# Mixture-of-experts stage of a two-layer transformer block: expert blocks of 64 slots on two column groups replaced by blocks of 32 slots on four

## The reference

```python
g_sel = argmax(tok @ gw + gb)                     # one of 4 groups
top_v, top_i = lax.top_k(e_logits of that group, 2)
w_sel = softmax(top_v) * p_g                      # two experts per token, 16 experts in all
for e in range(16):
    gu = tok @ w_gu[e]                            # 1024 -> 2 x 512
    act = silu(gu[:, :512]) * gu[:, 512:]
    y = y + combine[:, e:e + 1] * (act @ w_down[e])   # 512 -> 1024
```

| layer | tokens of experts 0 to 15 | blocks of 64 | blocks of 32 |
|---|---|---|---|
| 0 | 104, 55, 102, 67, 40, 60, 57, 45, 102, 93, 117, 70, 26, 34, 29, 23 | 23 | 40 (4,2,4,3,2,2,2,2,4,3,4,3,1,2,1,1) |
| 1 | 57, 30, 38, 21, 57, 29, 23, 71, 14, 19, 19, 16, 28, 20, 36, 34 | 17 | 23 (2,1,2,1,2,1,1,3,1,1,1,1,1,1,2,2) |

## Time and profile before

### The profile page before, as it was taken

The page is one execution under the profiler, slowest core; times in us unless marked ns, Lnnn a source line. Parts: engine busy times, 40 slices in busy tenths (PEclk is TensorE's granted clock), DMA queues, the critical chain, the costliest instruction groups (busy, mean ns, idle before and its releaser), DMA issues. The chain is left out here.

```text
span 1308.4 us, 15199 instructions
## 1 busy us (share of the span) xinstructions
PE 1125.2 (86%) x5396; PEld 575.0 (44%) x5397; DVE 289.6 (22%) x841; ACT 307.9 (24%) x732; POOL 145.8 (11%) x201
## 2 busy tenths in 40 slices
PE   5899999999996799879999469999995887888672
PEld 3344646656873333223333146666683322322220
DVE  1100064466115100000000051035715100000003
ACT  3211034454234011000111153125624100010002
POOL 0010033000000211111111110012000311111001
PEclk9999999999999799899999879999998998999997
DMA  9872548563406589999899841300047799999983
GB/s 350 299 278 111 229 157 315 212 246 130 193 1 265 170 311 330 352 391 365 323 334 354 312 156 65 118 11 1 1 193 284 268 329 394 390 376 393 394 358 112
DMA packets 92972, 322.89 MB, mean 247 GB/s; under 512 B 10954, under 2 KB 14068, under 8 KB 86644
## 3 DMA queue, kind: packets, MB, share of 16 engines
q1 hardware_dynamic: 70624, 279.19, 55.9%
q0 software_dynamic: 8032, 28.84, 6.7%
q10 hardware_dynamic: 14260, 14.10, 3.2%
HBM read 299.04 MB, written 23.07 MB: 246 GB/s over the span
## 5 line engine op out<-in xcount | busy, mean ns | idle before, releaser
L771 PE MATMUL psum<-weights,R 128*64 128x512 f32 x1280 | 309.9, 636 | 71.3 <-DMA weights<-in_exp_w_gu_dram 54.1
L771 PEld LDWEIGHTS psum<-weights,R 128*64 128x64 f32 x1280 | 100.1, 145 | 253.4 <-issue 253.0
L788 PE MATMUL psum<-weights,lat 128*64 128x512 f32 x592 | 135.2, 599 | 4.3 <-ACT lat L1093 4.3
L478 PE MATMUL psum<-hT,weights 128*128 128x512 f32 (+3 forms) x384 | 135.0, 511 | 2.4 <-ACT hT L935 2.4
L1503 DVE TENSOR_TENSOR lat<-lat,psum 128x256 f32<-128x256 f32 x42 | 17.7, 421 | 527.5 <-ACT lat L1089 527.5
L478 PEld LDWEIGHTS psum<-hT,weights 128*128 128x128 f32 (+1 forms) x384 | 68.5, 182 | 66.4 <-issue 57.5
L1089 ACT ACTIVATE lat<-psum 128x256 f32<-128x256 f32 x42 | 16.1, 383 | 311.5 <-PE psum L771 303.6
L1682 POOL COPY R<-R 64x1024 f32<-64x1024 f32 x40 | 41.3, 1032 | 400.0 <-PE psum L760 220.5
L1300 DVE TENSOR_REDUCE st<-psum 128x1 f32<-128x512 f32 (+1 forms) x96 | 56.9, 600 | 76.5 <-PE psum L588 36.0
L788 PEld LDWEIGHTS psum<-weights,lat 128*64 128x64 f32 x592 | 39.2, 136 | 70.6 <-issue 63.4
L1003 ACT ACTIVATE R<-psum,st 128x512 f32<-128x512 f32 (+1 forms) x78 | 48.0, 616 | 85.8 <-DVE st L1300 42.8
(11 more groups left out here) (224 smaller groups left out, 1081.8 us busy)
## 6 DMA issues: line engine op xcount, KB each, us to landing
weights<-in_exp_w_gu_dram SPq DMA_DIRECT2D x64, 2048.0 KB, 16.9
weights<-in_exp_w_down_dram SPq DMA_DIRECT2D x30, 2048.0 KB, 13.8
...
```

What stands on the lines that cost most here:

```text
L478: mm = nc.tensor.matmul(t[p0:p0 + m, lo:hi], w[:, k, col:col + m], hT[:, k, lo:hi], start=(k == 0), stop=(k == KD - 1))
L771: mm = nc.tensor.matmul(gu_ps[64 * j:64 * j + 64, :], xgT[:, k, :], w_gu[place][:, k, j, :, :], start=(k == 0), stop=(k == KD - 1), skip_g ...
L788: mm = nc.tensor.matmul(y_ps[64 * j:64 * j + 64, :], actT[:, kk % 2, (kk // 2) * 64:(kk // 2) * 64 + 64], w[kk][:, j * 512:(j + 1) * 512], ...
```

## The change

The block size becomes 32 slots, and each matmul of the expert stage uses one of four column groups of 32 with 256 moving columns in place of one of two groups with 512. The slots of a block are gathered as 128 pieces of 1 KB (a quarter of a row for each of the 128 partitions) instead of 64 rows of 4 KB; for this ACT writes the rows to `h_rows` in a permuted order. The gathered tile goes straight into one DVE transpose of 32x32 blocks, which gives `xgT`; POOL's copy, PE's transposes and DVE's copy out of PSUM go. The product of SiLU and up goes through a second DVE transpose in place of PE's two transposes and ACT's copy. The stores become four DMAs of 32 rows of 1 KB per block. PE now waits for `y_copied` and `act_ready` by name. Here is the diff, cut to its core:

```diff
@@ -38,7 +38,9 @@
-BLK = 64
+BLK = 32
+MORE = NTOK // BLK - 1
+QUADS = P // BLK
@@ -104,10 +106,12 @@
-put("more", np.tile(BLK * np.arange(1, 8) + 1, (P, 1)))
-put("count", np.tile(np.arange(BLK), (P, 1)))
+put("more", np.tile(BLK * np.arange(1, MORE + 1) + 1, (P, 1)))
+put("count", np.tile(np.arange(64), (P, 1)))
+put("place", np.tile(np.arange(P) % BLK, (P, 1)))
+put("quad", np.arange(P)[:, None] // BLK)
...
-    put(f"token{layer}", np.tile(np.arange(P)[:, None] + P * np.arange(tiles)[None], (1, 2)))
+    put(f"token{layer}", QUADS * np.tile(np.arange(P)[:, None] + P * np.arange(tiles)[None], (1, 2)))
@@ -173,7 +177,8 @@
-w_gu = [W[i][:, 0:8 * D].rearrange("p (k c h n) -> p k h c n", k=KD, c=2, h=2) for i in range(2)]
+w_gu = [W[i][:, 0:8 * D].rearrange("p (k c b j r) -> p k j c b r", k=KD, c=2, b=4, j=QUADS) for i in range(2)]
@@ -210,9 +215,10 @@
-xg_in = [R1[0:BLK, i * D:(i + 1) * D] for i in range(2)]
-xg = R1[0:BLK, 2 * D:3 * D]
-xgT = part(R1, 3 * D, KD * BLK, "p (k s) -> p k s", k=KD)
+xg = [part(R1, i * 256, 256) for i in range(2)]
+xgT = part(R1, 2 * 256, KD * BLK, "p (k s) -> p k s", k=KD)
@@ -229,9 +235,9 @@
-y_sb = [part(lat, i * 512, 512) for i in range(2)]
-silu_g, act_rows = (part(lat, 1024 + i * 256, 256) for i in range(2))
...
+y_sb = [part(lat, i * 256, 256) for i in range(2)]
+silu_g, act_rows = (part(lat, 512 + i * P, P) for i in range(2))
+actT = part(lat, 768, P, "p (b s) -> p b s", b=4)
@@ -270,18 +276,18 @@
-place_hot = part(lat, 0, 8 * BLK, "p (i s) -> p i s", i=8)
-block_id = part(lat, 8 * BLK, 8 * COLS, "p (i b) -> p i b", i=8)
+place_hot = part(lat, 0, 8 * P, "p (i s) -> p i s", i=8)
+block_id = part(lat, 3 * NTOK, 8 * COLS, "p (i b) -> p i b", i=8)
...
-slots = sb("slots", [BLK, COLS], I32)
-slot_col = sb("slot_col", [BLK, 2], I32)
+slots = sb("slots", [P, COLS], I32)
+slot_col = sb("slot_col", [P, 2], I32)
@@ -733,7 +739,8 @@
-mm = nc.tensor.matmul(t[0:BLK, 0:COLS], place_hot[:, i, :], block_id[:, i, :], start=(i == 0), stop=(i == 2 * nt - 1))
+mm = nc.tensor.matmul(t[:, 0:COLS], place_hot[:, i, :], block_id[:, i, :],
+                      start=(i == 0), stop=(i == 2 * nt - 1))
@@ -745,68 +752,52 @@
+for bank in (1, 3):
...
-def turn_x(g):
...
+gu_ps, y_ps = psum[:, 1, :], psum[:, 3, :]
+x_ready, act_ready, actT_ready = sem(f"x_ready{L}"), sem(f"act_ready{L}"), sem(f"actT_ready{L}")
+gu_done, y_done, y_copied = sem(f"gu_done{L}"), sem(f"y_done{L}"), sem(f"y_copied{L}")
+def gate_up(g, place, landed=None):
+    pe.wait_ge(act_ready, g + 1)
...
-        mm = nc.tensor.transpose(xt_ps[:, k * BLK:(k + 1) * BLK], xg[:, k * P:(k + 1) * P], ident[0:BLK, 0:BLK])
...
-        for j in range(2):
-            mm = nc.tensor.matmul(gu_ps[64 * j:64 * j + 64, :], xgT[:, k, :], w_gu[place][:, k, j, :, :],
+        for j in range(QUADS):
+            mm = nc.tensor.matmul(gu_ps[BLK * j:BLK * j + BLK, 0:256], xgT[:, k, :], w_gu[place][:, k, j, :, :, :],
...
-def turn_act(g):
...
-    for c in range(2):
-        mm = nc.tensor.transpose(at_ps[:, c * P:(c + 1) * P], act_rows[:, c * P:(c + 1) * P], ident)
...
+    pe.wait_ge(y_copied, g + 1)
+    pe.sem_inc(sem("pe_hold"), 1)
...
-        for j in range(2):
-            mm = nc.tensor.matmul(y_ps[64 * j:64 * j + 64, :],
...
+    for b in range(4):
+        for j in range(QUADS):
+            mm = nc.tensor.matmul(y_ps[BLK * j:BLK * j + BLK, 0:256], actT[:, b, :], w[b][:, j * 256:(j + 1) * 256],
+                                  start=(b == 0), stop=(b == 3), skip_group_check=True)
...
-turn_x(0)
...
+    n_blocks = pe.value_load(tabs[L][0:1, ds(pair * 2 + (T_NB + par), 1)], min_val=1, max_val=MORE + 1)
...
-    turn_x(start + 1)
...
-    turn_act(start)
@@ -818,9 +809,7 @@
-turn_x(g + 1)
...
-turn_act(g)
@@ -833,10 +822,9 @@
+pe.sem_inc(gu_done, 1)
@@ -1065,8 +1053,10 @@
-copy(S, rows[:, tt, half * 512:half * 512 + 512], ("hr", L, tt, half),
-     keys=[("h_tile", L, tt)] if half else [])
+src = read(act, "hr", L, tt, half)
+a(rows[:, tt, :].rearrange("p (a k r) -> p k a r", a=QUADS, k=KD)[:, 4 * half:4 * half + 4, :, :],
+  src.rearrange("p (k a r) -> p k a r", k=4, a=QUADS), ACT.Copy)\
+    .then_inc(*mark(S, ("read", "hr", L, tt, half), *([("h_tile", L, tt)] if half else [])))
@@ -1081,43 +1071,36 @@
+y_done, y_copied = sem(f"y_done{L}"), sem(f"y_copied{L}")
...
-    a(actT[:, :, :].rearrange("p c s -> p (c s)"), psum[:, 2, 0:256], ACT.Copy).then_inc(actT_ready, 1)
+    a(silu_g, psum[:, 1, 0:P], ACT.Silu).then_inc(silu_ready, 1)
...
-    a(y_sb[par], psum[:, 3, :], ACT.Copy).then_inc(y_copied, 1)
...
-    for j in range(2):
-        act.dma_start(y_rows[ds(n * BLK - BLK, BLK), j * 512:(j + 1) * 512], y_sb[par][64 * j:64 * j + 64, :])\
+    act.wait_ge(sem(f"y_stored{par}{L}"), ((n + 1) >> 1) * (16 * QUADS))
+    a(y_sb[par], psum[:, 3, 0:256], ACT.Copy).then_inc(y_copied, 1)
+    act.wait_ge(y_copied, n + 1)
+    for j in range(QUADS):
+        act.dma_start(y_rows[ds(n * BLK - BLK, BLK), j * 256:(j + 1) * 256], y_sb[par][BLK * j:BLK * j + BLK, :])\
...
+    act.sem_inc(sem(f"y_stored{par}{L}"), 16 * QUADS)
+act.sem_inc(y_copied, 1)
@@ -1448,9 +1431,9 @@
-step(tt_(cmp7[:, :, :], e16[:, 0, :].unsqueeze(2).to_broadcast([P, 16, 7]),
...
-step(red(e16[:, 1, :], cmp7[:, :, :], AX.X, ALU.add))
+step(tt_(more_of[:, :, :], e16[:, 0, :].unsqueeze(2).to_broadcast([P, 16, MORE]),
+         C("more").unsqueeze(1).to_broadcast([P, 16, MORE]), ALU.is_ge))
+step(red(e16[:, 1, :], more_of[:, :, :], AX.X, ALU.add))
@@ -1465,10 +1448,10 @@
-step(ts(spos_t[:, 1, 0:n2], spos[:, 0:n2], 6, None, ALU.logical_shift_right))
+step(ts(spos_t[:, 1, 0:n2], spos[:, 0:n2], 5, None, ALU.logical_shift_right))
...
-tt_(place_hot[:, 0:n2, :], spos_f[:, 0, 0:n2].unsqueeze(2).to_broadcast([P, n2, BLK]),
-    C("count")[:, 0:BLK].unsqueeze(1).to_broadcast([P, n2, BLK]), ALU.is_equal)
+tt_(place_hot[:, 0:n2, :], spos_f[:, 0, 0:n2].unsqueeze(2).to_broadcast([P, n2, P]),
+    C("place").unsqueeze(1).to_broadcast([P, n2, P]), ALU.is_equal)
@@ -1477,7 +1460,7 @@
-nc.vector.tensor_copy(slots[:, :], t[0:BLK, 0:COLS]).then_inc(*mark(S, ("read", "st", L), ("slots", L)))
+ts(slots[:, :], t[:, 0:COLS], C("quad"), None, ALU.add).then_inc(*mark(S, ("read", "st", L), ("slots", L)))
@@ -1487,22 +1470,36 @@
-    return nc.vector.tensor_copy(xgT[:, :, :].rearrange("p k s -> p (k s)"), psum[:, 0, :]).then_inc(x_ready, 1)
+x_ready, gu_done, silu_ready = sem(f"x_ready{L}"), sem(f"gu_done{L}"), sem(f"silu_ready{L}")
+act_ready, actT_ready, y_done = sem(f"act_ready{L}"), sem(f"actT_ready{L}"), sem(f"y_done{L}")
+def x_turn(par):
+    nc.vector.transpose(xgT[:, :, :].rearrange("p k s -> p (k s)"), xg[par]).then_inc(x_ready, 1)
+def block(g, par):
+    v.wait_ge(sem(f"gathered{1 - par}{L}"), ((g + 1) >> 1) * 16 + 16)
+    v.sem_inc(sem("v_hold"), 1)
+    v.wait_ge(gu_done, g + 1)
+    x_turn(1 - par)
+    v.wait_ge(silu_ready, g + 1)
+    tt_(act_rows, silu_g, psum[:, 1, P:2 * P], ALU.mult).then_inc(act_ready, 1)
+    if not isinstance(g, int) or g:
+        v.wait_ge(y_done, g)
+        v.sem_inc(sem("v_hold"), 1)
+    v.wait_ge(act_ready, g + 2)
+    nc.vector.transpose(actT[:, :, :].rearrange("p b s -> p (b s)"), act_rows).then_inc(actT_ready, 1)
+    v.wait_ge(actT_ready, g + 1)
...
+v.sem_inc(act_ready, 1)
+v.wait_ge(sem(f"gathered0{L}"), 16)
+x_turn(0)
+block(0, 0)
+block(1, 1)
+with v.Fori(1, (total + 1) >> 1) as pair:
...
+        block(pair * 2 + par, par)
@@ -1663,44 +1660,33 @@
+x_ready, col_ready = sem(f"x_ready{L}"), sem(f"col_ready{L}")
+h_parts = h_rows[L].rearrange("t (a c) -> (t a) c", a=QUADS)
...
+def gather(g, par):
...
+    g_.indirect_dma_start(xg[par], None, h_parts, bass.IndirectOffsetOnAxis(ap=slot_col[:, par:par + 1], axis=0))\
...
-def pass_on(g, par):
...
-    nc.gpsimd.tensor_copy(xg, xg_in[par]).then_inc(x_rows, 1)
...
-gather(1, 1, xg_in[1])
+gather(0, 0)
+gather(1, 1)
...
-gather(2, 0, xg_in[0])
-pass_on(1, 1)
-gather(3, 1, xg_in[1])
...
+pairs = (total + 1) >> 1
+with g_.Fori(0, pairs) as pair:
...
-        pass_on(pair * 2 + par, par)
-        gather(pair * 2 + (par + 2), par, xg_in[par])
-pass_on(pairs * 2 - 2, 0)
-pass_on(pairs * 2 - 1, 1)
+        g_.wait_ge(x_ready, pair * 2 + (par + 1))
+        g_.sem_inc(sem("hold"), 1)
+        gather(pair * 2 + (par + 2), par)
...
+    g_.wait_ge(sem(f"gathered{par}{L}"), pairs * 16 + 16)
+for par in range(2):
+    g_.wait_ge(sem(f"y_stored{par}{L}"), ((total + (1 - par)) >> 1) * (16 * QUADS) + 16 * QUADS)
```

More of the change, by code:

```diff
@@ L272, in hybrid_block @@
         r16 = sb("r16", [P, 6, 4, 16])
-        cmp7 = sb("cmp7", [P, 16, 7])
+        more_of = sb("more_of", [P, 16, MORE])
         e16 = sb("e16", [P, 5, 16])
@@ L746, in experts @@
             def experts(L):
-                for bank in range(4):
+                for bank in (1, 3):
                     pe.wait_ge(*at(*last_read[bank]))
-                xt_ps, gu_ps, at_ps, y_ps = (psum[:, b, :] for b in range(4))
```

(24 more changed lines are left out.)

40 lines of the change are left out of this document (removed).

## The result

The changed kernel takes 1257.68 us in the median of four runs (1254.14 to 1259.81), beside 1312.61 for the kernel before: a ratio of 0.9577, interval 0.9543 to 0.9611. The profiled execution took 1259.81 us, its span is 1258.0 (1308.4 before).

What follows compares the result with a forecast made beforehand. Layer 0 was taken as mostly PE-bound, layer 1 as bound by weight loads. Gains of 16.0 and 5.4 less 2.0, 0.5 and 2.0 gave 17 us: span 1308.4 to 1291.5, median 1295.4, range 1278 to 1325.

Steps and rivals of the forecast that it cites:

- Part 1, PE's block: Expert stages: four column groups side by side make a block of 32 take 5.34 us of PE, bounds 5.34 and 7.6.
- Part 2, the chain: DVE turns, product, ACT copy, store issues, gathers around a block: hidden under PE's gate/up and down, charged nothing.
- Part 3, DMA: Expert stages' transfers: 5.27 us per weight piece, gathers and stores 1.3 us per block of 32, bounds 0.8 and 2.5.
- The idle time: DMA engines in layer 0's expert stage: 30 us idle before, 5 after; in layer 1, 2 after.
- First loads and tails: Expert stages' ends: layer 0's first load at 456.0, tail 14.1 to 6.5 us; layer 1's at 1027.0, tail 15.8 to 11.9.
- rival 2: Expert stages' DMA: 1 KB packets cost only their bytes, 28 us less DMA over 57 blocks, total 1278; chance 0.12.
- Rival 3: POOL queue, both stages: gather packets stay dear, the 17 us gain gone at 0.3 us a block, up to 1326; chance 0.15.

Runs made afterwards that it cites:

- The longer down: Changed kernel with two of the four rounds of down repeated into a free bank, 0.86 us more PE per block: 1281.95 us, 0.9747 of the kernel before.
- the second gather: Changed kernel with every gather issued twice, the second into a spare tile, 0.131 MB more per block: 1274.12 us, 0.9697 of the kernel before.

## Why the prediction was wrong

By its own steps:

- **Part 1, PE's block: right.** 5.34 forecast, 5.18 measured. Pairs are 54 ns apart, and the nearest row, PE's transposes at 0.061, was no floor. So the 62 ns that the Trainium skill, "TensorE: Matmul & The Clock Gate", section "Wait — 56ns, not 53.3ns?", gives for matmuls that the sequencer's software decodes do not bind here.
- **Part 2, the chain: right.** 0.4, 0.3 and 0.4 us for the turn, the product and the copy, measured 0.45, 0.25 and 0.38; the four issues take 1.75, not 1.96. In layer 0's middle, where the rows above lie, nothing inside a block waits; over both stages PE waits five times for VectorE before L771, 9.1 us in all.
- **Part 3, DMA: this is the step that failed,** by the price of the side traffic and of a weight piece. "I take 1.3 us a block; bounds are 0.8 (by bytes alone) and 2.5": leaving all sides out shows 0.66 for a block of 32 in layer 1, and the queues' shares, worked as in the prediction, give 0.34 for a gather and 0.39 for its stores, 0.73. Both are below my lower bound. The term that was off is the gather's: "128 x 0.111 / 16 = 0.89 us", measured 0.32 to 0.34. Its premise, 128 packets of 1 KB, is what the trace refutes: there are 49, of 0.114 us in the mean. The stores' 0.45 was near. The price before, 1.60 for a block of 64, was about right (1.15 and 0.60 by leaving each out). But my lower bound halved it, and with it the surplus of gathers into 64 partitions, which does not come along to 128. "By bytes alone" should have been 0.262 MB at the rate of the strip's best slices, 410 GB/s: 0.64. And "5.27" for a piece was the weight packet as the gathers slowed it; the piece by itself takes 5.14.
- By the measured terms layer 0's busy part is 40 x 5.14 + 36 x 0.64 = 229 us and layer 1's 40 x 5.14 + 21 x 0.64 = 219; I had 258 and 238, and the traces show 232.6 and 219.4. That is 44 us of miss where the span missed by 33; the rest is given back by scatter and by the small terms below.
- **The idle time: right.** 30 us before and 5 after in layer 0; 26.6 and 4.6 measured. But I thought that PE had "time to spare" then and "no longer holds up the loads", though my own figures for a four-block expert (21.4 us of PE against 21.0 of DMA) did not say so. Measured, it is 4 x 5.18 = 20.7 against 3 x 5.14 + 4 x 0.64 = 18.0: there PE sets the pace, and the two weight buffers and the shorter experts between hide it. The longer down shows how little room is left.
- **First loads and tails.** In layer 0 the first load came 18.1 us after the start (18.9 forecast), in layer 1 8.2 (5.3). Tails are 8.4 and 13.9 us, for 6.5 and 11.9: the last down waits 1.20 for VectorE's turn, and the half gate_up before it took 3.56 us, where I had put 2.6.
- **Rivals.** It went as rival 2, to which I gave 0.12: the sides cost only their bytes. It was right in the price and not in the reason, as the gathers have no 1 KB packets. The stores have, and with small packets at the 0.0167 of the earlier trace rows one of theirs takes an estimated 0.042 us, where one of 2 KB took 0.083 in the earlier trace rows: half. The Trainium skill, "DMA: Bandwidth & Descriptors", section "Specifications", gives 512 B as the size from which transfers run at line rate, and these packets and the second gather's 0.32 us agree with it. I turned it down by "the gathers' dear packets in this trace", which were dear for another reason. Even the rival's 1278 was too long, as it carried the old price of a piece and took layer 0's gain to stop halfway. Rival 3, a gather above 1.2 us, is out.
